# Squares of the first norm on ScalarE, a logarithm in two parts, and another order of small tasks at the entry of a recurrence

## The chip, the cores and the metric

The kernel runs on one core of a Trainium2 chip. The metric is the device time of one execution in microseconds (us). The core has five engines with instruction queues of their own: TensorE (PE, matmuls), VectorE (DVE), ScalarE (ACT), GpSimd (POOL) and SyncE (SP, which here issues DMAs). They wait for one another through semaphores.

## The reference, cut to what matters

512 tokens and 16 meta tokens, 1024 wide, pass through two blocks in float32. What the change touches lies at the start of the first block and in the second one:

```python
h = rmsnorm(h_res, norm1_w[l])              # x * rsqrt(mean(x * x) + eps) * w
proj = h @ w_in[l]                          # q, k, v, z, b, a, ...
qkv = silu(depthwise_conv_centred(concat([q, k, v]), conv_w))   # 5 taps
beta = sigmoid(b_raw)
g = -exp(A_log) * softplus(a_raw + dt_bias) # log decay, needs log(1 + exp(-|.|))
# gated delta rule, forward and backward, chunks of tokens, 8 heads:
#   v_new = u - w S;  o = q_dec S + (q k^T * decay) v_new;  S = S * exp(g_last) + k_dec^T v_new
...
u = causal_depthwise_conv(a_val * sigmoid(a_glu), conv_w, conv_b)   # 31 taps, second block
d = pooled differences of b_val, times pool_w; yb = d * pool_scale * silu(b_gate)
```

## The kernel before

Tokens lie in the free dimension, channels in the 128 partitions. A weight "unit" is 8 tiles of 128x128. For each, SP loads w_raw, ACT rounds it to w_hi (`round_unit`, L384), POOL computes the remainder w_lo (`split_unit`, L390), and PE makes three products with the activations' own hi and lo parts (`gemm`, L402). Four units are in flight.

First norm: the products of units 0 and 1 (tiles k0, k1) use the unnormalized x times the norm's weight, u_hi and u_lo. POOL squares the tiles 0 to 2 of x (L2431), ACT the tiles 3 to 7 (L1743), DVE first makes u_lo (L2085) and then adds the squares (L2092), PE takes the mean (L1447) and then the lo products (L425). ACT takes the root (L1748), DVE the reciprocal (L2097); units 0 to 3 are scaled afterwards (`scaled`, L2104). For units from 4 on, DVE makes the normalized rows (`first_row`, L2107), ACT rounds them into hp_hi (`first_hi`, L1754) and POOL makes hp_lo (`first_lo`, L2436). ACT does k = 4 to 7 of these at the start of its step n = 3, POOL likewise.

Tile loop: 24 tiles of q, k and v, a unit each. For tile n ACT copies the product into cacc with the first tap (L1772), DVE adds four taps (L2124), ACT applies silu (L1763). The dictionary `SIDE` names small tasks for each step n, done by every engine that has a part in them: the gates' decay (`gd`, DVE's log1p, L1227 to L479), decay sums (`dk`, L1477), transposes of k and v (`kt`, `vt`), exponentials of a chunk pair (`pg`) and its key and query products (`pk`), meta tokens' state (`msa`, `msb`), parts of a triangular inverse on DVE (`sub`, L610, L613, L616). A chunk pair is half the heads of one chunk, 8 pairs in all. The results of `pg` and `pk` go through DRAM (`sp_pk`: d_at, d_kc, d_qd, d_p) because SBUF is full; the next `pg` on the buffer waits until the store has landed (`spilled`).

Recurrence: 16 slots, forward and backward in turn. A slot loads its matrices (L1026 to L1049), doubles the inverse (`pe_t`, `pe_yx`, `pe_y64`), multiplies by the state (`pe_ks`), solves (`pe_w`, L919, after DVE's `dve_r` and `dve_yc64`) and updates (`pe_ds`). Pairs 5 to 7 are prepared inside slots 0 to 2 (`PREP`). The order on each engine is the order in the program text.

Second block: DVE runs the 31-tap filter in 248 steps (L1218), spread by hand between other work: `BV_STEPS` after each tile of the pooled branch, five ahead of each of four pairs of yb (L2341), and `BG_STEPS` ahead of each tile of the bgate product.

Of the kernel before, what the change touches and what calls it, by code (L numbers as in the profile page):

```python
# [14 lines left out]
KT = D // P  # L15
# [4 lines left out]
H = 8  # L20
# [19 lines left out]
SQP = 3  # L40
# [19 lines left out]
BV_STEPS = [4, 4, 3, 15, 7, 10, 14, 34]  # L60
BG_STEPS = [6, 6, 6, 5, 5, 5, 0, 0]
# [7 lines left out]
for _name, _n, _k in PARAMS:  # L69
# [13 lines left out]
SIDE = {1: [("ba", 0)], 2: [("bat", 0)], 3: [("gd", 0)], 4: [("kt", 0)], 5: [("kt", 1), ("dk", 0)],  # L83
# [7 lines left out]
        24: [("pg", 4), ("vt", 3), ("vtm", 3), ("pkp", 4), ("msa", 1), ("msb", 1), ("pk", 4)]}  # L91
# [35 lines left out]
def build(nc, a, out):  # L127
    ctx = ExitStack()
    with ctx:
# [190 lines left out]
        sq = Signal(sem("s_sq"), n1=KT - SQP, q=H, z=H, out=KT, down=2 * KT, va=KT, mix=KT, lout=KT)  # L320
# [22 lines left out]
        pw = Signal(sem("s_pw"), n1=SQP, s=sum(j // 2 + 2 for j in range(4, KT)))  # L343
# [126 lines left out]
        def dve_gd(e):  # L470
            t = [tmpc[:, i, :] for i in range(4)]
            t0 = t[0].rearrange("p (c n) -> p c n", c=NB)
            ea = small[:, 32:48].unsqueeze(1).to_broadcast([P, NB, 16])
            e.wait_ge(*ga.at("ex", 1))
            n = log1p(e, dg, "ch", 3, t[1], t[2], t[3])
            e.scalar_tensor_tensor(t[0], t[0], 0.0, t[1], ALU.max, ALU.add).then_inc(dg.sem, 1)
            e.wait_ge(*dg.at("ch", n + 1))
            e.wait_ge(*ga.at("eA", 1))
            e.scalar_tensor_tensor(gdec[:], t0, -1.0, ea, ALU.mult, ALU.mult).then_inc(dg.sem, 1)  # L479
            for _ in range(20 - n - 2):  # L480
                e.sem_inc(dg.sem, 1)
# [742 lines left out]
        def log1p(e, sig, part, n, y, t1, t2):  # L1224

            c = [2.0 / (2 * k + 1) for k in range(SERIES)]
            e.tensor_scalar(t1, y, 2.0, None, ALU.add).then_inc(sig.sem, 1)  # L1227
            e.wait_ge(*sig.at(part, n + 1))
            e.reciprocal(t2, t1).then_inc(sig.sem, 1)
            e.wait_ge(*sig.at(part, n + 2))  # L1230
            e.tensor_tensor(y, y, t2, ALU.mult).then_inc(sig.sem, 1)
            e.wait_ge(*sig.at(part, n + 3))
            e.tensor_tensor(t1, y, y, ALU.mult).then_inc(sig.sem, 1)
            e.wait_ge(*sig.at(part, n + 4))
            e.tensor_scalar(t2, t1, c[SERIES - 1], None, ALU.mult).then_inc(sig.sem, 1)
            n += 5
            for k in range(SERIES - 2, 0, -1):
                e.wait_ge(*sig.at(part, n))
                e.scalar_tensor_tensor(t2, t2, c[k], t1, ALU.add, ALU.mult).then_inc(sig.sem, 1)
                n += 1  # L1240
            e.wait_ge(*sig.at(part, n))
            e.scalar_tensor_tensor(y, t2, c[0], y, ALU.add, ALU.mult).then_inc(sig.sem, 1)
            e.wait_ge(*sig.at(part, n + 1))
            return n + 1
# [188 lines left out]
        def pe_program(e):  # L1433
# [5 lines left out]
            for n in range(len(TILES) + 1):  # L1439
# [18 lines left out]
                for task, arg in SIDE.get(n, ()):  # L1458
# [27 lines left out]
                    if task == "pg":  # L1486
                        pe_pg(e, arg)
# [15 lines left out]
            pe_t(e, 0, 0, 32)  # L1503
            pe_yx(e, 0, 0)
            pe_t(e, 0, 0, 64)
            for q, (s, k) in enumerate(SLOTS):
                nx = SLOTS[q + 1] if q < 15 else None
                if q in PREP:
                    pe_pg(e, PREP[q])
                pe_ks(e, s, k)  # L1510
                pe_y64(e, s, k)
                if nx:
                    pe_t(e, *nx, 32)
                if q in ZAT:
                    pe_z(e, ZAT[q])
                if q in SCA:
                    pe_c(e, SCA[q])
                if q in SCB:
                    pe_b(e, SCB[q])
                if q in (10, 12):  # L1520
                    pe_on(e, q - 10)
                pe_w(e, s, k)
                if nx:
                    pe_yx(e, *nx)
                if q in ZAT:
                    pe_z(e, ZAT[q] + 1)
                if q in SCA:
                    pe_x(e, SCA[q])
                if q == 8:
                    pe_on_sum(e, 0)  # L1530
                if q in (10, 12):
                    pe_on(e, q - 9)
                if q in PREP:
                    pe_pk(e, PREP[q])
                pe_ds(e, s, k)
                if nx:
                    pe_t(e, *nx, 64)
# [193 lines left out]
        def act_program(e):  # L1731
# [4 lines left out]

            round_unit(e, 0)
# [4 lines left out]
            for k in range(SQP, KT):  # L1742
                e.activation(sqv[:, k, :], x_in[:, k, :], ACT.Square).then_inc(sq.sem, 1)  # L1743
# [3 lines left out]
            e.wait_ge(*dg.at("halo", 9))  # L1747
# [9 lines left out]
            for n in range(len(TILES) + 2):  # L1757
# [6 lines left out]
                if n < len(TILES):  # L1764
                    what, h = TILES[n]
                    b = 2 * (n % 2)
                    for k in ((), (), (0, 1, 2), (4, 5, 6, 7))[n] if n < 4 else ():
                        first_hi(k)
# [4 lines left out]
                    if n == 2:  # L1773
                        first_hi(3)
# [40 lines left out]
            act_tc(e, 0, 0, 32)  # L1815
            act_xc(e, 0, 0)
            act_tc(e, 0, 0, 64)
            for q, (s, k) in enumerate(SLOTS):
                nx = SLOTS[q + 1] if q < 15 else None
                act_kd(e, s, k)  # L1820
                if q in PREP:
                    act_pg(e, PREP[q])
# [4 lines left out]
                if nx:  # L1827
                    act_tc(e, *nx, 32)
                if q in ZAT:
                    act_z(e, ZAT[q])  # L1830
# [244 lines left out]
        def dve_program(e):  # L2075
# [10 lines left out]
            e.wait_ge(*pw.at("n1", 1))  # L2086
            for k in range(1, KT):
                e.wait_ge(*(pw.at("n1", k + 1) if k < SQP else sq.at("n1", k - SQP + 1)))
                if k > 1:
                    e.wait_ge(*ad.at("n1", k - 1))  # L2090
                s = pair(sqv[:, 0, :]) if k == 1 else ps[:, 6:8, 0:HALF]
                e.tensor_tensor(pair(cacc[:, 0, :]) if k == KT - 1 else ps[:, 6:8, 0:HALF], s, pair(sqv[:, k, :]), ALU.add).then_inc(ad.sem, 1)  # L2092
# [19 lines left out]
            for n in range(len(TILES) + 1):  # L2112
# [21 lines left out]
                for task, arg in SIDE.get(n, ()):  # L2134
                    if task == "bat":
                        dve_bat(e)
                    if task == "gd":
                        dve_gd(e)
# [14 lines left out]

            dve_yc32(e, 0, 0)
            for q, (s, k) in enumerate(SLOTS):
                nx = SLOTS[q + 1] if q < 15 else None
                if q in PREP:
                    dve_pg(e, PREP[q])
                dve_r(e, s, k)
                dve_yc64(e, s, k)  # L2160
                if q in (4, 5):
                    sub_part(e, 1, 3 * (q - 4) + 1)
                dve_vn(e, s, k)
                if q in SCB:
# [5 lines left out]
                if q in PREP:  # L2170
                    dve_pk(e, PREP[q])
# [3 lines left out]
                dve_o(e, s, k)  # L2175
                if q in (3, 4, 5):
# [89 lines left out]
            n = log1p(e, dg, "lam", 3, t[1], t[2], t[3])  # L2266
# [160 lines left out]
        def pool_program(e):  # L2427
            split_unit(e, 0)
            for k in range(SQP):
                e.wait_ge(s_x[k // 2], 16 if k > 1 else 32)  # L2430
                e.tensor_tensor(sqv[:, k, :], x_in[:, k, :], x_in[:, k, :], ALU.mult).then_inc(pw.sem, 1)  # L2431
# [7 lines left out]
            for n in range(len(TILES) + 1):  # L2439
                if n == 3:  # L2440
                    for k in range(4, KT):
                        first_lo(k)
                if n < len(TILES):
                    split_unit(e, n + 2)
                if n == 2:
                    for k in range(4):
# [12 lines left out]
            e.memset(oT[:], 0.0).then_inc(pz.sem, 1)  # L2459
            for q, (s, k) in enumerate(SLOTS):  # L2460
# [234 lines left out]
```

## Time and profile before

| | |
|---|---|
| three runs | 1849.55, 1853.29, 1853.92 us |
| median | 1853.29 us |
| the profiled execution | 1849.43 us, of which the span is 1847.6 us |
| mean granted PE clock | 0.972 of full speed |
| PE busy | 1755.8 us (95% of the span) |
| DVE busy | 842.5 us (46%) |
| ACT busy | 667.1 us (36%) |
| POOL busy | 866.8 us (47%) |

PE is the busiest engine by far, and the chain of work that ended last is PE's for 74% of the span. Idle time of another engine costs nothing unless PE, or a chain that PE hangs on, waits for it. A clock of 0.5 in a stretch means that PE's matmuls run at 1.2 instead of 2.4 GHz there.

### The profile page before, as it was taken

What the parts mean: (1) busy time and instruction counts of PE and PEld (TensorE: products, weight loads), DVE (VectorE), ACT (ScalarE), POOL (GpSimd) and SP (SyncE); (2) the same over time, 40 slices, a digit from 0 to 9 for tenths busy, and PEclk for the clock granted to TensorE, in tenths of its full rate; (3) what the DMA queues carried; (4) which work ended last, traced back from release to release, by engine and by line L of the source; (5) the groups of instructions that cost most, each with busy time, mean ns of one, the idle gap of its engine ahead of it and who ended that gap; (6) DMA issues with size and microseconds to landing.
All of it is one profiled execution on the core that took longest, in us unless ns stands there. A gap on an engine that the chain in (4) does not pass through costs nothing.

```text
span 1847.6 us, 22825 instructions
## 1 busy us (share of the span) xinstructions
PE 1755.8 (95%) x9151; PEld 1478.5 (80%) x9151; DVE 842.5 (46%) x1338; ACT 667.1 (36%) x978; POOL 866.8 (47%) x485
## 2 busy tenths in 40 slices
PE   7799979999999999999999999989999999999987
PEld 7789878898998888877888878868887788877766
DVE  7677944833433300222111121128999933357732
ACT  5456533333232322234222232232233244356551
POOL 4345533322333644544555554444477445456552
PEclk9899978999999999999999999989999989999999
DMA  4367267454322224322322223323233222222222
GB/s 172 101 207 214 75 179 217 135 157 135 121 86 77 96 91 137 95 95 85 101 93 91 93 90 103 102 68 103 92 91 103 80 69 90 88 97 92 92 69 80
DMA packets 120145, 201.41 MB, mean 109 GB/s; under 512 B 32448, under 2 KB 71512, under 8 KB 120040
## 3 DMA queue, kind: packets, MB, share of 16 engines
q1 hardware_dynamic: 118552, 197.47, 33.6%
q10 hardware_dynamic: 1488, 2.48, 0.4%
q8 instruction: 73, 1.20, 0.3%
q14 instruction: 32, 0.26, 0.0%
HBM read 170.46 MB, written 29.46 MB: 108 GB/s over the span
## 4 chain that ended last, share of the span: by engine, by line
PE 74%; DVE 6%; POOL 2%; issue 2%; ACT 1%; DMA 0%; SPq 0%; DVEq 0%; ACTq 0%; POOLq 0%
PE ps L402 60%; PE ps L1723 3%; DVE ps L1218 2%; PE ps L873 1%; POOL w_lo L390 1%; PE ps L919 1%; PE ps L883 1%; POOL tmp L2524 1%; PE ps L881 1%; PE ps L926 1%; PE ps L913 1%; PE ps L930 1%; PE ps L905 1%; PE ps L891 1%; DVE ps L1337 1%
## 5 line engine op out<-in xcount | busy, mean ns | idle before, releaser
L390 POOL TENSOR_TENSOR w_lo<-w_raw,w_hi 128x1024 fp32r<-128x1024 f32 x264 | 634.4, 2411 | 574.5 <-ACT w_hi L384 574.2
L402 PE MATMUL ps<-hp_hi,w_hi 128*128 128x512 f32 (+2 forms) x1664 | 557.1, 362 | 3.8 <-DVE cacc L2124 1.5
L402 PE MATMUL ps<-hp_lo,w_hi 128*128 128x512 f32 (+2 forms) x1664 | 552.0, 359 | 0.0
L402 PE MATMUL ps<-hp_hi,w_lo 128*128 128x512 f32 (+2 forms) x1664 | 551.8, 359 | 0.0
L402 PEld LDWEIGHTS ps<-hp_hi,w_hi 128*128 128x128 f32 x1664 | 296.5, 190 | 60.2 <-issue 7.9
L384 ACT ACTIVATE w_hi<-w_raw 128x1024 fp32r<-128x1024 f32 x264 | 277.8, 1054 | 172.2 <-DMA w_raw<-in_w 164.1
L402 PEld LDWEIGHTS ps<-hp_lo,w_hi 128*128 128x128 f32 x1664 | 296.1, 189 | 50.4 <-issue 1.7
L402 PEld LDWEIGHTS ps<-hp_hi,w_lo 128*128 128x128 f32 x1664 | 296.0, 189 | 48.1
L1218 DVE SCALAR_TENSOR_TENSOR ps<-u_in,par,ps 128x511 f32<-128x511 f32 (+14 forms) x240 | 177.3, 739 | 7.7
L2124 DVE SCALAR_TENSOR_TENSOR cacc<-ps,par,cacc 128x528 f32<-128x528 f32 x96 | 73.6, 767 | 42.1 <-ACT cacc L1772 39.4
L2503 POOL TENSOR_TENSOR y_lo<-tmp,y_hi 128x512 fp32r<-128x512 f32 x22 | 28.4, 1290 | 105.6 <-ACT y_hi L1917 105.6
L402 PE MATMUL ps<-y_hi,w_hi 128*128 128x512 f32 x176 | 69.6, 396 | 1.5 <-DVE tmp L2255 1.5
L402 PE MATMUL ps<-y_lo,w_hi 128*128 128x512 f32 x176 | 69.5, 395 | 0.0
L402 PE MATMUL ps<-y_hi,w_lo 128*128 128x512 f32 x176 | 69.5, 395 | 0.0
L1914 ACT ACTIVATE tmp<-tmp 128x512 f32<-128x512 f32 x22 | 13.9, 632 | 150.6 <-DVE tmp L2248 150.6
L402 PE MATMUL ps<-mx_hi,w_hi 128*128 128x512 f32 x144 | 59.2, 411 | 4.8 <-DVE yb L2341 4.8
L2250 DVE TENSOR_TENSOR ps<-ps,tmp 128x512 f32<-128x512 f32 x22 | 15.4, 699 | 103.8 <-PE ps L402 103.8
L402 PE MATMUL ps<-mx_lo,w_hi 128*128 128x512 f32 x144 | 58.5, 406 | 0.0
L402 PE MATMUL ps<-mx_hi,w_lo 128*128 128x512 f32 x144 | 58.3, 405 | 0.0
L2248 DVE TENSOR_TENSOR tmp<-tmp,ps 128x512 f32<-128x512 f32 x22 | 15.1, 687 | 92.4 <-PE ps L402 85.7
L1008 POOL TENSOR_TENSOR KC<-st,tabs 128x512 f32<-128x512 f32 x16 | 16.9, 1053 | 84.3 <-PE ps L905 71.4
L2277 DVE TENSOR_TENSOR x<-x,ps 128x512 f32<-128x512 f32 x8 | 5.5, 686 | 102.2 <-PE ps L402 102.2
(397 smaller groups left out, 2602.8 us busy)
## 6 DMA issues: line engine op xcount, KB each, us to landing
w_raw<-in_w SPq DMA_DIRECT2D x264, 512.0 KB, 3.5
d_y<-zero SPq DMA_DIRECT2D x6, 688.0 KB, 6.0
d_x<-zero SPq DMA_DIRECT2D x6, 688.0 KB, 5.9
d_at<-at SPq DMA_DIRECT2D x16, 256.0 KB, 3.1
d_kc<-kc SPq DMA_DIRECT2D x16, 256.0 KB, 3.2
d_qd<-eg SPq DMA_DIRECT2D x16, 256.0 KB, 3.2
d_p<-dec SPq DMA_DIRECT2D x16, 256.0 KB, 3.3
AT<-d_at SPq DMA_DIRECT2D x16, 256.0 KB, 6.2
```

Source lines behind the costliest of these rows:

```text
L384: e.activation(w_hi[:, u % RAW, :], w_raw[:, u % RAW, :], ACT.Copy).then_inc(s_hi, 1)
L390: e.tensor_tensor(w_lo[:, u % RAW, :], w_raw[:, u % RAW, :], w_hi[:, u % RAW, :].bitcast(F32), ALU.subtract).then_inc(s_lo, 1)
L402: mm = e.matmul(ov, w, r[:, k, t0:t1], start=(first and n == 0 and p3 == 0), stop=(last and n == len(tiles) - 1 and p3 == 2))
L873: mm = e.matmul(bankv(LB[s], P, P)[:, u], SQ[s]["AT"][:, u], SQ[s]["X"][:, u], start=True, stop=True)
L881: e.matmul(half_cols(LB[s], 0)[:, u], T[:, u], blocks(Y, 1 - s)[:, u], start=True, stop=True)
L883: mm = e.matmul(half_cols(LB[s], 1)[:, u], Y[:, u], blocks(T, s)[:, u], start=True, stop=True)
L891: mm = e.matmul(bankv(LB[s], P, 64)[:, u], T[:, u], Y[:, u, c], start=True, stop=True)
L905: mm = e.matmul(bankv(QBK[s], P, P)[:, u], SQ[s]["KC"][:, u], S[:, u], start=True, stop=True)
L1218: e.scalar_tensor_tensor(acc[:, t:SEQ], u_in[:, k, 0:SEQ - t], w, acc[:, t:SEQ], ALU.mult, ALU.add).then_inc(cl.sem, 1)
L1723: mm = e.matmul(ps[:, LBANK[j], :], w, r[:, k, :], start=(k == 0 and p3 == 0), stop=(k == LT - 1 and p3 == 2))
L2124: e.scalar_tensor_tensor(acc, ps[:, b:b + 2, t:t + HALF], pcol(QKV[what][0], h, t), acc, ALU.mult, ALU.add).then_inc(cv.sem, 1)
L2503: e.tensor_tensor(y_lo[:, j - 1, :], row(2 + (j - 1) % 2), y_hi[:, j - 1, :].bitcast(F32), ALU.subtract).then_inc(lo.sem, 1)
```

## The change

1. The three squares on POOL go; ACT squares all eight tiles. ACT does a square root of one column at its very start, and no longer waits for DVE's clearing ahead of the real root.
2. DVE's log1p for the gates is cut in two: five operations (`log1p_ratio`, task `gda`) at step 3, and the rest (`log1p_series` and two more, task `gdb`) at step 4 behind the transposes' copies `kt`. The logarithm of lambda in the second block calls both, one behind the other.
3. ACT rounds hp_hi 3 to 7 in one go in step 2, POOL makes hp_lo 0 to 7 in one go in step 2.
4. Of pair 4's tasks at step 24 only PE's part of `pg` stays. The other engines' parts, `pk`, `msa` and `msb` of the second half are spread over the first operations of the recurrence.
5. In slots 0 to 2 the preparation of pairs 5 to 7 (`pg`, `pk`) moves behind the slot's own operations on PE, ACT and DVE. SP's order is the same.
6. `BV_STEPS` has 28 instead of 34 steps for the last tile; `BG_STEPS` has six more, in tiles 3, 4 and 6 as the lists show.

```diff
-BV_STEPS = [4, 4, 3, 15, 7, 10, 14, 34]
-BG_STEPS = [6, 6, 6, 5, 5, 5, 0, 0]
+BV_STEPS = [4, 4, 3, 15, 7, 10, 14, 28]
+BG_STEPS = [6, 6, 6, 6, 6, 5, 4, 0]
-SIDE = {1: [("ba", 0)], 2: [("bat", 0)], 3: [("gd", 0)], 4: [("kt", 0)], 5: [("kt", 1), ("dk", 0)],
+SIDE = {1: [("ba", 0)], 2: [("bat", 0)], 3: [("gda", 0)], 4: [("kt", 0), ("gdb", 0)], 5: [("kt", 1), ("dk", 0)],
...
-        24: [("pg", 4), ("vt", 3), ("vtm", 3), ("pkp", 4), ("msa", 1), ("msb", 1), ("pk", 4)]}
+        24: [("pgp", 4), ("vt", 3), ("vtm", 3)]}
...
+        def dve_gda(e):
+            e.wait_ge(*ga.at("ex", 1))
+            log1p_ratio(e, dg, "ch", 3, tmpc[:, 1, :], tmpc[:, 2, :], tmpc[:, 3, :])
+        def dve_gdb(e):
...
+            n = log1p_series(e, dg, "ch", 8, t[1], t[2], t[3])
...
             pe_t(e, 0, 0, 32)
+            pe_msa(e, 1)
             pe_yx(e, 0, 0)
+            pe_msb(e, 1)
             pe_t(e, 0, 0, 64)
...
-                if q in PREP:
-                    pe_pg(e, PREP[q])
+                if q == 0:
+                    e.wait_ge(*m_st.at(1))
                 pe_ks(e, s, k)
+                if q == 0:
+                    pe_pk(e, 4)
                 pe_y64(e, s, k)
...
                 pe_w(e, s, k)
+                if q in PREP:
+                    pe_pg(e, PREP[q])
...
+                pe_ds(e, s, k)
                 if q in PREP:
                     pe_pk(e, PREP[q])
-                pe_ds(e, s, k)
...
+            e.wait_ge(*dg.at("halo", 9))
+            e.activation(rrow[:, 0:1], rrow[:, 0:1], ACT.Sqrt)
             round_unit(e, 0)
...
-            for k in range(SQP, KT):
+            for k in range(KT):
                 e.activation(sqv[:, k, :], x_in[:, k, :], ACT.Square).then_inc(sq.sem, 1)
...
-                    for k in ((), (), (0, 1, 2), (4, 5, 6, 7))[n] if n < 4 else ():
+                    for k in (0, 1, 2) if n == 2 else ():
                         first_hi(k)
...
                     if n == 2:
-                        first_hi(3)
+                        for k in range(3, KT):
+                            first_hi(k)
...
             act_tc(e, 0, 0, 32)
+            act_msa(e, 1)
             act_xc(e, 0, 0)
+            act_msb(e, 1)
+            act_pg(e, 4)
             act_tc(e, 0, 0, 64)
...
+            dve_pg(e, 4)
             dve_yc32(e, 0, 0)
...
                 dve_r(e, s, k)
+                if q == 0:
+                    dve_pk(e, 4)
                 dve_yc64(e, s, k)
...
                 dve_vn(e, s, k)
+                if q in PREP:
+                    dve_pg(e, PREP[q])
...
                 dve_s(e, s, k)
                 dve_o(e, s, k)
+                if q in PREP:
+                    dve_pk(e, PREP[q])
...
-            for k in range(SQP):
-                e.wait_ge(s_x[k // 2], 16 if k > 1 else 32)
-                e.tensor_tensor(sqv[:, k, :], x_in[:, k, :], x_in[:, k, :], ALU.mult).then_inc(pw.sem, 1)
...
                 if n == 2:
-                    for k in range(4):
+                    for k in range(KT):
                         first_lo(k)
...
             e.memset(oT[:], 0.0).then_inc(pz.sem, 1)
+            pool_pk(e, 4)
```

## Rows read from the trace of the kernel before

**Rows 1.** Waits of PE, whole span: engine, line, waited for: us, times, longest.

```profile
PE ps L637 <- ACT qT L1763: 6.2, 1, 6.2
...
PE ps L402 <- DVE yb L2341: 5.7, 2, 4.8
...
PE ps L417 <- ACT hp_hi L1754: 4.6, 1, 4.6
PE ps L1447 <- DVE cacc L2092: 4.6, 1, 4.6
```

**Rows 2.** Windows, PE first in each row; PEclk is the granted clock.

```profile
22.00:26.00 4.00, 2.51 (x7) 0.60 0.00 0
...
82.00:86.00 4.00, 4.00 (x18) 0.50 0.00 0
...
110.00:200.00 90.00, 86.98 (x681) 79.96 (x681) 68.40 (x139) 50.82 (x71) 50.14 (x47) 0.99 0.63 192
```

**Rows 3.** One line's instructions, u_lo on DVE: durations min/median/max in ns.

```profile
L2085 DVE SCALAR_TENSOR_TENSOR u_lo<-x_in,par,u_hi x8: 756/1508/2902, 7.0 to 17.0; 128x528 fp32r<-128x528 f32 x8
```

**Rows 4.** Timeline of the first 32 us: start us, us, engine, line, operation.

```profile
13.40 2.76 ACT L1743 ACTIVATE sqv<-x_in 128x528 f32<-128x528 f32 x5
...
13.57 2.98 POOL L390 TENSOR_TENSOR w_lo<-w_raw,w_hi 128x1024 fp32r<-128x1024 f32 x1 [1.20 <-ACT w_hi L384]
...
18.53 4.00 DVE L2092 TENSOR_TENSOR ps<-ps,sqv 128x528 f32<-128x528 f32 x5
...
23.49 2.10 PE L1447 MATMUL ps<-cacc,cf 128*128 128x264 f32 x4 [4.61 <-DVE cacc L2092]
...
25.01 6.40 PE L425 MATMUL ps<-u_lo,w_hi 128*128 128x268 f32 x32
```

**Rows 5.** Timeline from 47 to 91 us.

```profile
47.98 2.78 DVE L2107 SCALAR_TENSOR_TENSOR hf<-x_in,par,ps 128x528 f32<-128x528 f32 x4
...
51.15 0.27 ACT L1786 ACTIVATE beta<-beta 128x80 f32<-128x80 f32 x1 [4.39 <-DVE beta L463]
...
55.37 0.64 ACT L1763 ACTIVATE kT<-cacc 128x528 f32<-128x528 f32 x1
...
58.76 3.18 DVE L2124 SCALAR_TENSOR_TENSOR cacc<-ps,par,cacc 128x528 f32<-128x528 f32 x4 [6.35 <-ACT cacc L1772]
61.86 2.40 DVE L1227 TENSOR_SCALAR tmpc<-tmpc 128x80 f32<-128x80 f32 x1
...
64.15 4.76 POOL L390 TENSOR_TENSOR w_lo<-w_raw,w_hi 128x1024 fp32r<-128x1024 f32 x2
...
69.28 1.90 DVE L1239 SCALAR_TENSOR_TENSOR tmpc<-tmpc 128x80 f32<-128x80 f32 x7
...
75.91 1.94 PE L637 MATMUL ps<-cf,kT 128*128 128x128 f32 x8 [6.24 <-ACT qT L1763]
77.65 0.90 PE L1477 MATMUL ps<-gdec,cf 128*128 128x32 f32 x4
...
90.63 0.60 PE L643 MATMUL ps<-cf,kT 128*16 128x128 f32 x4
```

**Rows 6.** Timeline where the tiles pass into the recurrence, 238 to 315 us.

```profile
238.90 1.03 DVE L616 COPY raw<-inv 128x1024 f32<-128x1024 f32 x1
...
249.68 0.38 SPq L1029 DMA_DIRECT2D X<-d_x  x1
...
252.22 1.13 DVE L560 SCALAR_TENSOR_TENSOR at<-ps,b,dec 128x128 f32<-128x128 f32 x4 [10.22 <-ACT st L840]
...
252.79 2.05 PE L873 MATMUL ps<-X,AT 128*128 128x128 f32 x8 [1.24 <-issue]
...
283.31 1.13 DVE L522 SCALAR_TENSOR_TENSOR dec<-ps,tabs,cf 128x128 f32<-128x128 f32 x4 [3.39 <-DMA d_p<-dec]
...
285.63 2.04 PE L919 MATMUL ps<-TR,Y 128*128 128x128 f32 x8 [3.61 <-DVE Y L974]
...
314.82 0.48 PE L402 MATMUL ps<-hp_hi,w_hi 128*128 128x512 f32 x1
```

**Rows 7.** Timeline of DVE near the end of the bval tiles, 31-tap filter.

```profile
1421.47 10.16 DVE L1218 SCALAR_TENSOR_TENSOR ps<-u_in,par,ps 128x511 f32<-128x511 f32 x13
```

## What I predict, and why

> **What bounds the kernel now.** I first read the page: TensorE (PE) is busy 95% of the span, so time can only come from PE's remaining waits and from stretches where its clock is low. Then the view of PE's waits, longest first [rows 1]. The reader is to see that three of its long waits lie in the places this change touches: 4.6 us for the sum of the first norm's squares, 4.6 us for hp_hi and 6.2 us for a silu near 75 us, and that a fourth, 5.7 us in two pieces for yb near 1433, lies where the step lists act. Then the timeline of each engine around each wait, and the windows for PE's clock. In between PE is the bound: from 110 to 200 us it works 86.98 of 90 us [rows 2], so what is won ahead of it arrives as a shift of all that follows. The sum is made on the profiled execution, 1849.4 us; the median shown is 1853.3, with one run at 1849.6, so the profile is one of the quicker executions.
>
> **1. First norm's squares on ACT.** Removed: three squares on POOL; each of them stretches the u_lo operations beside it on DVE from 0.76 to about 1.5 us, and the last one, beside POOL's w_lo(1), takes 2.90 [rows 3]. So DVE finishes u_lo near 17.7 and only then adds. Added: three squares on ACT at 2.76 / 5 = 0.55 us. All eight begin at 13.40 [rows 4]; the second is ready at 14.5, the eighth at 17.8. u_lo without POOL follows ACT and is done near 13.3. The adds come every 0.80 us (4.00 / 5) and need seven: from 14.5 they would end at 20.2. The first add reads two SBUF tensors while POOL writes w_lo(1) from about 13.5 to 15.9. If it is held to the end, the last add ends near 20.9; before, PE got it at 23.49 [rows 4]. Gain 2.4 to 3.1; I take 2.4, because u_lo's 2.90 shows such a hold. The Trainium skill (GPSIMD Engine Reference, section 8, Key points) says that GpSimd shares its SBUF interfaces with VectorE and contends with its instructions that have two SBUF inputs; by that rule the sum takes 2.4, without it 3.1, and the trace agrees with the rule (0.76 against 2.90).
> PE's gap before the mean also shrinks, from 4.6 to about 2.2 us. Before, its clock stood at 0.60 in 22 to 26 us [rows 2], the four mean matmuls took 2.10 and the 32 lo matmuls 6.40 [rows 4]; at the full level I estimate half of the one and 4.0 for the other. PE then runs without a gap to 51.9, so it could win 3.4 more, but DVE's chain (root, reciprocal, first tap) only moves by the mean's 1.0 and then by what PE hands it, about 2.0 in all. Full clock: 4.4. I take **-4.0** (ends -2.2 and -4.6). The early square root moves a table load to a place where ACT waits for its first DMA: nothing, and the load's old place was inside ACT's wait for the mean.
>
> **2. Logarithm in two parts, hp_hi and hp_lo in one run.** In the times of before: DVE's rows for k = 4 to 7 are there by 50.8 [rows 5]. ACT now rounds them at once, by 51.4, and POOL's four remainders end near 53.8 instead of 61. PE's unit 4 then needs no wait: 49.8 to 55.9. Its 4.6 us go, but unit 5 needs tile 3's taps, so what is late next is DVE's tile 3. Its price: ACT starts the sigmoid after 51.4 plus a table load, 52.7; from there to the silu took 4.22 us (51.15 to 55.37), so the silu is at 56.9, the copy into cacc at 57.5, DVE's taps from 58.2 to 61.3 instead of 58.76 to 61.9. Unit 5 starts at 61.35 rather than 63.46, after a gap of 4.4 us and so at the low clock at first: I let it end at 69.0.
> DVE then: before, the log's first operation waited 2.40 us for POOL [rows 5], and the whole took 61.86 to 71.99. Now w_lo(6) is over by 61.5, w_lo(7) begins near 63.6, and the five operations of the first part (0.2 us or so each, 0.65 for the reciprocal) fit in between: 63.1. Taps of tile 4 to 66.2, two copies into k_tok (1.28) to 67.5, the second part's ten operations at 0.27 (7 in 1.90) to 70.2. PE's transposes of kt(1) wait for those copies, which are now there before unit 5 ends, and run behind it to 70.0 instead of starting at 75.91 [rows 5]; its decay sums start at 70.2 instead of 77.65. They and unit 6 took until 90.5, at clock 0.50 [rows 2, 5]: 4.6 and 8.4 us. At the full level I estimate 2.5 and 6.1, so unit 6 ends at 78.8; at the low level throughout, 83.2. Gain 7.2 to 11.7. PE has worked since 61.35, so I take **-10.5**. Behind unit 6 ACT, DVE and POOL are free sooner as well, and the weight loads are tied to PE's own signals, so the whole is a shift.
>
> **3. Order of small tasks.** Pair 4's key products, the memory state of the second half (msa, msb) and their ACT, DVE and POOL parts leave the end of the tile loop. But the recurrence starts on its transfers: X is issued at 249.68 behind the scatters and PE starts at 252.79 on it [rows 6]; the scatters hang on DVE's last copy of the substitution, 238.90 to 239.9 [rows 6], which the change leaves alone. So the moved work was in a cover that now stays empty, for 13 us. What it costs inside: msa(1) and msb(1) fall in PE's waits for ACT, 0.2 us. DVE's four operations of pk(4), two groups of four at 1.13 us [rows 6] and two products of some 0.7, together 3.75, now stand between r and yc64 of slot 0, so W of slot 0 waits from about 269.1 to 273.2, against 269.3 before: +3.9. SP's eight stores of pair 4 wait for them too (256 to 262 before, 270 to 275 now), and behind them SP's loads of slot 2, needed 10 us later, and the P buffer that DVE's next dec waits for. Against this, PE's pg(5) to pg(7), DVE's pk and POOL's pk now come at the end of their slots, so r and yc64 of the next slot are released by the pk in front of them: slot 1's W waited 3.61 us, and ran at 2.04 us for eight instead of some 1.1, because dec waited 3.39 us for d_p [rows 6]. I followed the slots with these durations: with PE at the full level the z products, at 314.82 before [rows 6], start 2.3 us sooner; if the 4.1 us wait drops the clock for some ten us, as after 285.63, 1.9 later. Every wait of that length in the trace was followed by the low level. I take **+1** (ends -3 and +6, for a spill landing late once more). The Trainium skill (TensorE: Matmul & The Clock Gate, HAM oscillation) describes a loop in which each wait between bursts returns the array to half rate; by it the term is +1.9.
>
> **4. Steps of the 31-tap filter.** Six steps leave the eighth bval tile for the later bgate ones. Behind them DVE produces yb, on which PE waits 4.8 and 0.9 us. A step costs 10.16 / 13 = 0.78 us [rows 7], six 4.7; DVE is the bound from there to the first bgate unit. The steps reappear where DVE waited 2 to 5 us per tile for ACT (from 1472 on), so their cover holds; tile 7's sum, due when PE ends bgate 7, is done some 6 us ahead. **-4.6** (ends -2.6, if bgate 0 now runs at the low clock after the shorter waits, and -4.8). The split logarithm of lambda has the same operations: nothing.
>
> **Sum.** -4.0 - 10.5 + 1 - 4.6 = -18.1 on 1849.4 gives 1831.3. Since the shown median stands higher than its profile, I forecast 1833.
>
> **Rivals.** (a) The clock does not come back: the mean, the decay sums and unit 6 stay at 1.2 GHz, as in 82 to 86 us [rows 2], and slot 0's stall lowers it again: -2.4 for part 1, -7.2 for 2, +3 for 3 and -3 for 4 are -9.6, so with the same 1.7 for the median 1841.5. For it: the decay sums are tiny matmuls, in which the clock stayed low before. Against it: no gap stands before them now. (b) The first part of the logarithm misses its window between w_lo(6) and w_lo(7), by 0.5 us or more, and is again held some 2.4 us, and once more by what follows: -18.1 + 5 gives 1838. The margin is thin. (c) The entry becomes the bound: each of slots 0 to 2 pays what slot 1 did before (stall 3.6, low clock about 5), slot 0 also its pk(4) (3.8) and the moved products at the low clock (about 5.7), and the spills of P land late, 4.6 us in each. That is some 26 + 10 less the one stall that was there (8.7), plus 14: 41 at the very worst; the other parts give 19.1, so it decides from 19.1 + 5.6 = 24.7 us on, and at 30 it gives 1862. For it: slot 1 shows the pattern. Against it: in slots 0 and 2 as they were, the same waits stayed below 1 us. (d) The log's gain stays but the filter's is taken by the next wait: yb's wait only moves to a bgate unit, 1838.
>
> **Chances.** Forecast 0.50, (a) 0.22, (b) 0.13, (c) 0.04, (d) 0.06, more gain than forecast 0.05. The likeliest case alone reaches from 1825 to 1838; the range with (a) and (b), and 2 us for which execution is the median, is 1823 to 1844. 0.3% of the time is 5.6 us, about what a measurement can tell from none. Faster by more 0.92, within 0.05, slower 0.03.
>
> **What would show it.** Adds begin near 14.5 and the mean near 21; no wait of PE inside unit 4; a wait of some 4 us in front of unit 5; log operations in two groups with none over 1 us; decay sums some 11 us earlier (7.5 and part 1's shift); PE idle from about 240 to 252 less the shift; a wait of W in slot 0 near 4 us; the wait for yb under 2.5 us in each piece. The prediction is wrong if a w_lo holds a log operation, if the clock stays low through unit 6, or if the slots behind 252 take over 6 us more.

## The result, and the profile after

The changed kernel takes 1831.9 us in the median (1831.81 to 1837.01, 4 runs), the kernel before 1851.4 (1849.54 to 1853.92, 4 runs): ratio 0.9901, 95% interval 0.9878 to 0.9924. The profiled execution took 1831.8 us, its span is 1830.0 us at a mean granted clock of 0.976. Predicted were 1833 us and a range of 1823 to 1844. Four more executions of the same kernel on a later occasion had a median of 1837.3 beside 1852.6 for the kernel before, so the gain is 19.5 us by the first occasion and 15.3 by the second. Both occasions hold executions near 1832 and near 1837 us; what lies between these two figures is told below.

PE's waits of the changed kernel, longest first (engine, line, waited for: us, times, longest), answer to [rows 1]:

```profile
PE ps L875 <- issue: 12.8, 1, 12.8
...
PE ps L921 <- DVE Y L976: 6.2, 4, 4.0
PE ps L401 <- DVE cacc L2137: 6.1, 2, 4.7
...
PE ps L401 <- DVE yb L2360: 3.5, 2, 2.1
...
PE ps L1450 <- DVE cacc L2105: 3.3, 1, 3.3
```

The wait for hp_hi in unit 4 and the one for the silu near 75 us are gone. New are 4.7 us in front of unit 5 (cacc) and 4.0 us in slot 0 (Y), both foretold. The wait for the mean has gone from 4.6 to 3.3 us, the one for yb from 5.7 to 3.5.

First norm, timeline of the changed kernel, against [rows 3, 4]:

```profile
6.76 6.53 DVE L2099 SCALAR_TENSOR_TENSOR u_lo<-x_in,par,u_hi 128x528 fp32r<-128x528 f32 x8 [4.69 <-ACT u_hi L1751]
...
12.96 4.37 ACT L1754 ACTIVATE sqv<-x_in 128x528 f32<-128x528 f32 x8
13.14 2.43 POOL L389 TENSOR_TENSOR w_lo<-w_raw,w_hi 128x1024 fp32r<-128x1024 f32 x1 [5.17 <-ACT w_hi L383]
14.16 1.99 DVE L2105 TENSOR_TENSOR ps<-sqv 128x528 f32<-128x528 f32 x1 [0.86 <-ACT sqv L1754]
...
21.21 1.72 PE L1450 MATMUL ps<-cacc,cf 128*128 128x264 f32 x4 [3.32 <-DVE cacc L2105]
22.35 5.54 PE L424 MATMUL ps<-u_lo,w_hi 128*128 128x268 f32 x32
```

The eight u_lo take 6.53 us where they took over 10. The first add begins at 14.16 and is held to 16.15, past the end of POOL's w_lo(1) at 15.57: the hold that I had taken. The same add took 0.70 us in the kernel before, where it ran from 17.72 with POOL idle. The mean starts at 21.21 instead of 23.49.

Units 5 and 6, timeline of the changed kernel, against [rows 5]:

```profile
55.71 2.35 POOL L389 TENSOR_TENSOR w_lo<-w_raw,w_hi 128x1024 fp32r<-128x1024 f32 x1 [0.24 <-ACT w_hi L383]
...
57.81 0.30 DVE L1228 TENSOR_SCALAR tmpc<-tmpc 128x80 f32<-128x80 f32 x1
57.95 0.81 PE L401 MATMUL ps<-hp_hi,w_hi 128*128 128x268 f32 x2 [4.67 <-DVE cacc L2137]
...
59.39 0.20 DVE L1236 TENSOR_SCALAR tmpc<-tmpc 128x80 f32<-128x80 f32 x1
...
63.79 1.89 DVE L1242 SCALAR_TENSOR_TENSOR tmpc<-tmpc 128x80 f32<-128x80 f32 x7
...
66.08 1.04 PE L639 MATMUL ps<-cf,kT 128*128 128x128 f32 x8
66.96 0.53 PE L1480 MATMUL ps<-gdec,cf 128*128 128x32 f32 x4
...
75.59 0.60 PE L645 MATMUL ps<-cf,kT 128*16 128x128 f32 x4
```

The first part of the logarithm (57.81 to 59.59) starts 0.25 us before w_lo(6) is over (58.06) and ends 0.6 us before w_lo(7) begins (60.19). The decay sums start at 66.96 instead of 77.65, 10.7 us sooner. The transposes behind unit 6 start at 75.59 instead of 90.63. Windows of the changed kernel (PE, its weight loads, DVE, ACT, POOL; then granted clock, DMA share, GB/s), against [rows 2]:

```profile
22.00:26.00 4.00, 4.00 (x22) 3.79 (x21) 2.50 (x3) 0.70 (x1) 0.00 (x0) 0.62 0.02 4
56.00:64.00 8.00, 6.05 (x32) 6.05 (x33) 7.69 (x15) 2.83 (x4) 4.43 (x2) 0.59 0.23 84
64.00:90.00 26.00, 25.93 (x209) 25.43 (x207) 16.50 (x33) 16.91 (x24) 4.77 (x2) 1.00 0.49 142
```

The granted clock is 1.00 (2.4 GHz) in all of 64 to 90 us, through decay sums and unit 6, where it had been at 0.50 (1.2 GHz) from the decay sums at 77.65 to near 88 us, in unit 6.

The entry of the recurrence, PE's timeline, against [rows 6]:

```profile
237.35 2.05 PE L875 MATMUL ps<-X,AT 128*128 128x128 f32 x8 [12.75 <-issue]
239.32 1.89 PE L818 MATMUL ps<-v_met,m_dec 16*16 16x128 f32 x8
...
244.74 2.07 PE L828 MATMUL ps<-v_met,k_met 16*128 16x128 f32 x8
...
251.21 1.06 PE L507 MATMUL ps<-kT 128*128 128x128 f32 x8
252.10 1.06 PE L512 MATMUL ps<-qT,kT 128*128 128x128 f32 x8
...
258.92 2.05 PE L921 MATMUL ps<-TR,Y 128*128 128x128 f32 x8 [3.98 <-DVE Y L976]
260.76 3.48 PE L498 MATMUL ps<-cf,gdec 128*128 128x128 f32 x16
...
274.52 1.13 PE L921 MATMUL ps<-TR,Y 128*128 128x128 f32 x8 [0.45 <-DVE Y L976]
...
287.58 1.13 PE L921 MATMUL ps<-TR,Y 128*128 128x128 f32 x8 [0.32 <-DVE Y L976]
...
300.08 0.48 PE L401 MATMUL ps<-hp_hi,w_hi 128*128 128x512 f32 x1
```

PE idles for 12.75 us, starts 15.4 us sooner than before (252.79), loses 3.98 in slot 0, and no longer the 3.61 of slot 1. L818 and L828 are PE's moved msa(1) and msb(1), L507 and L512 its moved products of pair 4. The z products start 14.7 us sooner.

DVE's 31-tap filter ahead of yb, and PE's two waits behind it, timelines of the changed kernel, against [rows 7]:

```profile
1406.78 5.47 DVE L1220 SCALAR_TENSOR_TENSOR ps<-u_in,par,ps 128x511 f32<-128x511 f32 x7
...
1418.95 0.50 PE L401 MATMUL ps<-mx_hi,w_hi 128*128 128x512 f32 x1 [2.14 <-DVE yb L2360]
...
1423.41 0.50 PE L401 MATMUL ps<-hp_hi,w_hi 128*128 128x512 f32 x1 [1.40 <-DVE yb L2360]
```

Seven steps stand where 13 did (10.16 us). The first bgate unit starts 19.3 us sooner than before (1442.73).

Of these 19.3 us only 17.6 reach the end. The loss of 2.1 us has one place (0.4 is won back in small pieces behind it): 64 matmuls of one column each (the variance of a later norm, L1670 before, L1679 after). They took 9.41 us from 1509.79 before and take 11.53 now:

```profile
1490.44 11.53 PE L1679 MATMUL ps<-cf,tmp 128*128 128x1 f32 x64
```

PE is busy all the while; only the clock differs. Windows there, columns as above, first of the kernel before, then of the changed one:

```profile
1512.00:1514.00 2.00, 2.00 (x20) 2.00 (x19) 0.00 (x0) 0.00 (x0) 0.00 (x0) 1.00 0.31 125
1514.00:1516.00 2.00, 2.00 (x13) 2.00 (x12) 0.00 (x0) 0.00 (x0) 0.00 (x0) 0.61 0.03 8
```

```profile
1492.00:1494.00 2.00, 2.00 (x15) 2.00 (x14) 0.00 (x0) 0.00 (x0) 0.00 (x0) 0.69 0.62 242
1494.00:1502.00 8.00, 7.97 (x38) 7.88 (x37) 0.00 (x0) 0.00 (x0) 0.00 (x0) 0.50 0.01 2
```

The clock falls about 5 us into the group before, and less than 3 us into it after.

### The profile page after: what moved, and what is told of

Read it like the earlier page. It is cut to its first block, busy times and chain, and to the rows that moved or that the text cites. A ratio compares the mean times of both kernels' runs of the same rounds, so it can differ in the third digit from the quotient of the medians.

```text
span 1830.0 us, 22824 instructions
## 1 busy us (share of the span) xinstructions
PE 1744.6 (95%) x9151; PEld 1469.1 (80%) x9151; DVE 836.0 (46%) x1338; ACT 668.1 (37%) x981; POOL 861.5 (47%) x482
## 4 chain that ended last, share of the span: by engine, by line
PE 80%; DVE 11%; ACT 3%; issue 2%; POOL 2%; DMA 1%; SPq 0%; DVEq 0%; ACTq 0%; POOLq 0%
PE ps L401 63%; PE ps L1732 3%; DVE cacc L2137 2%; DVE ps L1220 2%; PE ps L875 2%; POOL w_lo L389 1%; PE ps L921 1%; POOL tmp L2538 1%; DVE inv L615 1%; PE ps L928 1%; PE ps L885 1%; PE ps L907 1%; PE ps L883 1%; PE ps L915 1%; PE ps L932 1%
## 5 line engine op out<-in xcount | busy, mean ns | idle before, releaser
L2268 DVE TENSOR_TENSOR ps<-ps,tmp 128x512 f32<-128x512 f32 x22 | 15.4, 699 | 103.9 <-PE ps L401 103.9
L943 ACT ACTIVATE TR<-ps 128x512 f32<-128x512 f32 x32 | 19.1, 597 | 91.4 <-PE ps L875 91.4
```

The costliest lines, as they stand in the source:

```text
L943: e.activation(SQ[s]["TR"][:], bankv(LB[s], P, P), ACT.Copy).then_inc(q_tc[s].sem, 1)
```

## The experiments

A shift is how much sooner the same PE instruction starts than in the kernel before, in two profiled executions. Some shift can stand there already ahead of the part in question, where the clock rose or fell at another point; where it matters it is given too. Each part alone on the kernel before came first (the kernel before had 1852.6 us there, 28 runs, 1848.19 to 1859.09).

**Squares alone.** The whole first part of the change: ACT squares all eight tiles, POOL none, and the early square root is in.

```diff
+            e.wait_ge(*dg.at("halo", 9))
+            e.activation(rrow[:, 0:1], rrow[:, 0:1], ACT.Sqrt)
...
-            for k in range(SQP, KT):
+            for k in range(KT):
                 e.activation(sqv[:, k, :], x_in[:, k, :], ACT.Square).then_inc(sq.sem, 1)
...
-            for k in range(SQP):
-                e.wait_ge(s_x[k // 2], 16 if k > 1 else 32)
-                e.tensor_tensor(sqv[:, k, :], x_in[:, k, :], x_in[:, k, :], ALU.mult).then_inc(pw.sem, 1)
```

> The kernel before with the first part of the change alone (all eight squares on ACT, early square root). Theory A (POOL's three squares stretched u_lo and so the sum of squares, and the shorter gap lets PE's clock come back sooner): the mean's products start near 21.2 instead of 23.49, unit 2 near 33.7 instead of 37.2, and the 3.5 us pass through to the end: ratio near 0.998. Rival: the shift is eaten by PE's next wait, for hp_hi inside unit 4, which grows from 4.6 to about 8 us, and the time stays as before.

Measured: 1847.65 us, ratio 0.9972 (0.9959 to 0.9986). Mean at 21.20, all that follows 3.7 us sooner up to unit 4, where the wait for hp_hi grows from 4.6 to 5.4 us. From there to the decay sums the shift is 2.5 to 3.0 us, and behind unit 6 it is 4.1, since the clock came back 1 us sooner there. So hp_hi takes about 0.8 us and not the whole; how much of the 3.7 is left behind it, 2.5 to 4.1 us, depends on the clock. Squares and early square root were not taken apart.

**hp in one run, alone, and the logarithm cut in two, alone.**

```diff
-                    for k in ((), (), (0, 1, 2), (4, 5, 6, 7))[n] if n < 4 else ():
+                    for k in (0, 1, 2) if n == 2 else ():
...
-                        first_hi(3)
+                        for k in range(3, KT):
+                            first_hi(k)
...
-                if n == 3:
-                    for k in range(4, KT):
-                        first_lo(k)
...
-                    for k in range(4):
+                    for k in range(KT):
                         first_lo(k)
```

The second one calls the two halves of the function as in the change:

```diff
-3: [("gd", 0)], 4: [("kt", 0)],
+3: [("gda", 0)], 4: [("kt", 0), ("gdb", 0)],
```

> The kernel before with hp_hi 3 to 7 and hp_lo 0 to 7 each in one run in step 2, the logarithm whole. Theory A (the logarithm was slow because POOL's w_lo(6) and w_lo(7) ran beside it; moving POOL's remainders forward takes them apart): no wait in unit 4, the logarithm takes some 4.5 us instead of 10.1, the decay sums start at 71 to 72 instead of 77.65, gain 9 to 11 us, ratio near 0.995. Rival B (the cut of the logarithm is what gains): only the earlier unit 5 is won, some 2 us, ratio 0.999, with log operations still over 1.5 us.

> The kernel before with the logarithm cut in two alone. Theory A: the first part still meets w_lo(6) and w_lo(7) and is held as before (operations of 1.6 to 2.4 us), only the second part leaves the way of tile 4's taps; the decay sums start 0 to 3 us sooner, ratio 0.998 to 1.000. Rival B: the decay sums start near 70, gain 8 us or more, ratio 0.995.

hp alone: 1845.05 us, ratio 0.9956 (0.9938 to 0.9974), shift 6.5 us behind unit 6, of which 0.3 stood there ahead of unit 4, so 6.2 by the part: less than the 9 to 11 expected. The first part of the logarithm is free (0.20 to 0.65 us an operation), but the whole now runs on in one piece, and its series of seven falls beside the next w_lo, as DVE and POOL of this kernel show:

```profile
62.88 3.94 DVE L1239 SCALAR_TENSOR_TENSOR tmpc<-tmpc 128x80 f32<-128x80 f32 x7
...
63.44 2.45 POOL L390 TENSOR_TENSOR w_lo<-w_raw,w_hi 128x1024 fp32r<-128x1024 f32 x1 [2.13 <-ACT w_hi L384]
```

Seven operations take 3.94 us instead of 1.89. And it still stands ahead of tile 4's taps and, behind them, the first copy into k_tok, on which PE's transposes wait 1.78 us. (The profile puts this wait down to qT, which ends at about the same time; by the program, L635, it is the copy.)

The cut alone: 1848.07 us, ratio 0.9978 (0.9964 to 0.9991), decay sums 2.6 us sooner, as expected, and 2.5 behind unit 6; ahead of unit 4 a shift of 1.2 had stood there, which is no work of this part. DVE of this kernel shows why no more:

```profile
60.66 2.41 DVE L1229 TENSOR_SCALAR tmpc<-tmpc 128x80 f32<-128x80 f32 x1
63.11 0.65 DVE L1231 RECIPROCAL tmpc<-tmpc 128x80 f32<-128x80 f32 x1
63.79 1.68 DVE L1233 TENSOR_TENSOR tmpc<-tmpc 128x80 f32<-128x80 f32 x1
65.50 2.31 DVE L1235 TENSOR_TENSOR tmpc<-tmpc 128x80 f32<-128x80 f32 x1
```

Three of the first part's five operations are held by POOL, which works from 59.72 (w_lo(6)) to 67.7 with little pause since its hp_lo came late.

**Both together, without the rest** (both diffs above).

> The kernel before with the logarithm cut in two and with hp_hi and hp_lo in one run, nothing else. Theory A (the two halves need each other: the merged hp work frees POOL, so the first part of the logarithm is no longer held, and the cut lets the second part run behind the copies of kt): log operations of the first part under 0.7 us each, decay sums near 70, unit 6 over near 79, 10 to 12 us sooner than before, ratio 0.994. Rival B (the halves only add, as they were run alone: 6.2 and 2.5 us): decay sums near 69 to 72 and 8 to 9 us, ratio 0.9955. Rival C (the surplus came from the first norm's earlier end): the shift behind unit 6 is at most 9 us, with a POOL subtraction beside the first part.

1840.78 us (1836.64 to 1845.09, 6 runs) against 1852.28, ratio 0.9936 (0.9922 to 0.9950). First part 60.87 to 62.65 without a hold, series at 66.84 in 1.89 us, decay sums at 70.25, shift behind unit 6 10.2 us. Singly the shifts were 6.5 and 2.5, together 9.0; less what stood there ahead of unit 4 (0.5 here, 0.3 and 1.2 there) it is 9.8 against 6.2 + 1.3 = 7.5. So the two halves give 1.2 to 2.3 us more together than one by one. That is theory A, at its lower edge: B's ratio of 0.9955 lies outside the interval, and no log operation is over 0.7 us. C's 9 us is passed by little. In this execution the clock was still at 0.79 in 72 to 80 us. In the first profile of the full change it was 1.00 and the part gave 11.5; in the repeat told below, the same program, it gave 9.6, so this difference lies in the clock of the execution and not in the other parts.

**Step lists alone.**

```diff
-BV_STEPS = [4, 4, 3, 15, 7, 10, 14, 34]
-BG_STEPS = [6, 6, 6, 5, 5, 5, 0, 0]
+BV_STEPS = [4, 4, 3, 15, 7, 10, 14, 28]
+BG_STEPS = [6, 6, 6, 6, 6, 5, 4, 0]
```

> The kernel before with the two step lists alone. Theory A (DVE's filter steps hold yb, and yb holds PE): the first bgate unit starts 4.6 us sooner, of which 0 to 2.1 us are given back where the one-column products of the variance run longer at the low clock; ratio 0.9975 to 0.9986. Rival D (the wait only moves into a later bgate unit): ratio 1.000.

1848.95 us, ratio 0.9981 (0.9968 to 0.9994). The first bgate unit gains 4.6 us on the kernel before. In this execution that only makes up for 4.6 us lost ahead of it, most of it by clock falls near 550 to 590 us, so the unit starts at the same time in both. The waits for yb are 3.5 instead of 5.7 us; the other 2.4 us lie in PE's work there, at which the clock now stays at 1.00:

```profile
1428.00:1440.00 12.00, 9.73 (x41) 1.00 0.55 176
```

The same window of the kernel before is at 0.72. The one-column products begin at 1509.72, at the same time as before (1509.79), and take 10.81 us instead of 9.41: 1.4 us is given back.

The next four were timed beside one another, and so beside the changed kernel itself, whose median was 1837.3 us there (the kernel before had 1852.6, 7 runs):

**The old entry.** All of the third part undone, the rest of the change kept.

> The changed kernel with the old order of small tasks at the entry of the recurrence (pair 4 whole at the end of the tile loop, preparation of pairs 5 to 7 ahead of the slots' own work). Theory A (the new order loses about as much with pair 4 in slot 0 as it wins in slot 1): the first z products at the same time within 1.5 us, the wait of W in slot 0 gone, that in slot 1 back at some 3.6 us with the low clock behind it; time within 1.5 us of the changed kernel. Rival C (the entry costs): 3 us or more quicker than the changed kernel. Rival E (the entry is where part of the gain comes from): 3 us or more slower.

1835.09 us (1832.22 to 1839.29), ratio 0.9902 (0.9879 to 0.9924). From the transposes of v ahead of the entry (223.18 in the changed kernel) to the z products it takes 0.9 us less than the changed kernel. PE waits again 3.62 us in slot 1 and 1.28 in slot 2, but not in slot 0. Theory A holds by the trace: the third part as a whole moves the z products by less than a microsecond. The medians, 1835.09 against 1837.3, can't tell so little.

**Pair 4 back in its cover.** Only SIDE[24] and pair 4's tasks are as before; pairs 5 to 7 keep the new order in their slots.

```diff
-        24: [("pgp", 4), ("vt", 3), ("vtm", 3)]}
+        24: [("pg", 4), ("vt", 3), ("vtm", 3), ("pkp", 4), ("msa", 1), ("msb", 1), ("pk", 4)]}
...
-            pe_msa(e, 1)
             pe_yx(e, 0, 0)
-            pe_msb(e, 1)
...
-                if q == 0:
-                    pe_pk(e, 4)
...
```

The parts of ACT, DVE and POOL go back in the same way.

> The changed kernel, but pair 4's exponentials and products and the second half's memory state go back to the end of the tile loop; the new order for pairs 5 to 7 stays. Theory A: the work lies in the 12.8 us in which PE waits for the recurrence's first load, slot 0 has no wait of 4 us and no low clock behind it, and slot 1 keeps its gain: the first z products start 5 to 8 us sooner, time 1824 to 1827 us. Rival F (pair 4's stores and loads collide with the slots' loads, or its DVE work delays the first load): the first load lands later, or dec waits for its buffer, and no more than 2 us are won.

1825.72 us (1824.87 to 1829.53), ratio 0.9860 (0.9841 to 0.9879): the quickest kernel of this study, 6 us ahead of the changed one's first median and 11.6 ahead of the one beside it. PE's timeline of this version:

```profile
242.04 2.08 PE L875 MATMUL ps<-X,AT 128*128 128x128 f32 x8
...
255.78 1.13 PE L921 MATMUL ps<-TR,Y 128*128 128x128 f32 x8 [0.32 <-DVE Y L976]
...
268.98 1.13 PE L921 MATMUL ps<-TR,Y 128*128 128x128 f32 x8 [0.45 <-DVE Y L976]
...
294.54 0.48 PE L401 MATMUL ps<-hp_hi,w_hi 128*128 128x512 f32 x1
```

No W waits over half a microsecond, and from X to z are 52.5 us instead of 62.7 (300.08 - 237.35). PE works 6.41 us of 226 to 238 where the changed kernel works 0.65. From the transposes of v to z it is 9.3 us quicker than the changed kernel, and 8.5 quicker than the old entry. So the third part is two changes of opposite sign: the new order of pairs 5 to 7 in their slots saves 8.5 us, and taking pair 4 out of its cover costs 9.3 (with the new order in place; without it this was not run).

The rows of both kernels say where the 9.3 us go. The wait of W in slot 0 is 3.98 instead of 0.32 us (3.7). Slot 0 behind it, to the next W, runs 2.4 us longer, because the clock is low from that wait to 264 us. The moved msa(1) and msb(1) take 3.8 us at 1.2 GHz and fill waits of 1.5 that stood at their places (2.3). The moved products of pair 4 take 1.8 us, at full clock. Against this, the first doubling (X) comes 0.9 us sooner.

**Three steps back** into the eighth bval tile (31, with six, six, six, six, six, six and no others in the bgate list).

> The changed kernel with 31 instead of 28 filter steps behind the last bval tile (three fewer behind). Theory A: the first bgate unit starts 3 x 0.77 = 2.3 us later than in the changed kernel. If the one-column products for the variance are then not caught earlier by the low clock, part or all of it comes back: they take 9.4 to 11.5 us, so the time is 0.2 to 2.5 us longer than the changed kernel's. Rival D: no change in the first bgate unit, the wait was taken up elsewhere.

1834.31 us (1833.61 to 1838.38), ratio 0.9907 (0.9888 to 0.9926): not told apart from the changed kernel in time. In the trace the waits for yb are 4.6 us instead of 3.5, the first bgate unit starts 4.8 us later, of which 2.5 already stood there from clock falls, so 2.3 by the three steps, as expected, and the one-column products take 10.16 us, between those of the two lists.

**The changed kernel once more.**

> The changed kernel once more, beside the others on the same chip. Theory A and all rivals: 1832 us; the products for the variance near 11.5 us where the profile is like the first one, and another length wherever the clock falls at another point.

1837.3 us (1832.8 to 1837.69), ratio 0.9913 (0.9894 to 0.9932); its profile has a span of 1835.6 us, 5.6 more than the first. Compared instruction by instruction with the first, the difference arises in pieces: 1.6 us before 28 us, 1.9 in the decay sums and unit 6, 0.8 near 216, 1.2 between 250 and 300, 0.3 behind. Windows of the first execution and of this one (PE busy, granted clock, DMA share, GB/s):

```profile
72.00:76.00 4.00, 4.00 (x36) 1.00 0.00 0
212.00:220.00 8.00, 7.31 (x59) 1.00 0.13 40
```

```profile
72.00:76.00 4.00, 4.00 (x22) 0.59 0.40 149
212.00:220.00 8.00, 6.63 (x40) 0.79 0.15 61
```

The same program, the same matmuls, and a clock that falls in one execution and not in the other.

**ACT's gate operations behind tile 3**, on the version with pair 4 in its cover: the sigmoid and the two exponentials of step 2 go to step 3, behind the copy of tile 3 into cacc.

```diff
-                    if task == "bat":
+                    if task == "gda":
                         e.wait_ge(*dg.at("b", 1))
                         e.activation(beta[:], beta[:], ACT.Sigmoid).then_inc(ga.sem, 1)
```

> The version that keeps pair 4 in its cover, and ACT's three gate operations (a sigmoid, two exponentials, with two table loads) behind the copy of tile 3 into cacc instead of ahead of it. Theory A (the wait of 4.7 us in front of unit 5 hangs on ACT's gate operations, and what is late next is the second part of the logarithm): no wait in front of unit 5; PE waits some 2 to 4 us for k_tok and the decay sums instead; decay sums 2 to 3 us sooner; end 1822 to 1824 against 1826. Rival B (the table loads are not what unit 5 waits for, or w_lo is held instead): the wait stays above 3 us and the time is the same. Rival C (the first part of the logarithm now falls beside the subtraction of w_lo and is held 2 us): decay sums no sooner, 1826 or later.

1826.62 us (1825.36 to 1830.92), ratio 0.9858 (0.9843 to 0.9872) on a third occasion, so no gain is seen on pair 4 in its cover (1825.72). PE's and DVE's rows of this version:

```profile
55.45 0.52 PE L401 MATMUL ps<-hp_hi,w_hi 128*128 128x268 f32 x2 [2.09 <-DVE cacc L2128]
...
56.69 2.32 DVE L1234 TENSOR_TENSOR tmpc<-tmpc 128x80 f32<-128x80 f32 x1
...
63.07 1.23 PE L639 MATMUL ps<-cf,kT 128*128 128x128 f32 x8 [1.37 <-ACT qT L1767]
66.21 1.06 PE L1480 MATMUL ps<-gdec,cf 128*128 128x32 f32 x4 [1.92 <-DVE gdec L481]
```

Unit 5's wait falls from 4.7 to 2.1 us and it starts 3.8 us sooner than with pair 4 in its cover (1.2 of which stood there already), so just over half of the wait did hang on ACT's gate operations. But one operation of the first part is held 2.32 us by w_lo(6), PE waits 1.4 and 1.9 us further on, and the decay sums start 2.3 us sooner, but behind them the clock is low again (their first four matmuls take 1.06 us, at full clock 0.53): by 75 us both versions are level, and the 1.2 us that stood there are lost too. The wait was split, not removed. C came nearest, with its hold and its time, though the decay sums do start sooner.

## Why the prediction came out right, point by point

**Sum.** Predicted -18.1 on the profiled 1849.4, measured -17.6. By terms: part 1 -3.5 for -4.0, part 2 -11.5 for -10.5, part 3 +0.3 for +1, part 4 -4.6 for -4.6, then +2.1 that no term had, and -0.4 in small pieces behind. The forecast of 1833 lies between the medians of the two occasions, 1831.9 and 1837.3. That the sum is met within 0.5 us is in part luck: its terms are off by +0.5, -1.0, -0.7, 0, +2.1 and -0.4, which cancel, and in the repeat parts 1 and 2 gave 2.0 and 9.6 instead of 3.5 and 11.5, with the same program.

**Part 1** was right in its mechanism. The 3.1 us that the sum of squares would give without a hold did not come: 2.28 did, for the 2.4 taken. About 0.4 of them are the execution's: ACT began its squares at 12.96 instead of 13.40. In the five profiles with the old first norm the mean starts at 23.47 to 23.54, in the seven with the new one at 21.14 to 22.03. By the Trainium skill (GPSIMD Engine Reference, section 8, Key points), POOL contends with VectorE instructions that have two SBUF inputs; the trace agrees, with 1.99 us for the first add beside w_lo(1) and 0.70 for the same add with POOL idle in the kernel before. PE's gap before the mean shrank to 3.3 us only and not to 2.2, because PE's work ahead of it ended 1.0 us sooner as well. The half microsecond missing lies in the clock, which came back later in the lo products (5.54 us) than I had counted.

**Part 2** was right in each step: no wait in unit 4; 4.67 us in front of unit 5 (4.4 predicted); log operations of at most 0.65 us; transposes of kt(1) directly behind unit 5; decay sums 10.7 us sooner (11 predicted). The size lay near the upper end because the clock was at its full level from 64 us on; in four of the other profiles of both halves it fell once more in unit 6, and the part gave 9.6 to 9.8 us. The price of -10.5 lies between the two. Rival (b), the missed window, did not occur in the full change, but its mechanism is real: the cut alone has three operations held, hp alone a series at twice its time, and the kernel with ACT's gate operations behind tile 3 one operation of 2.32 us. In the full change the first part ends 0.6 us ahead of w_lo(7).

**Part 3** was right as a sum, and in part by luck: W of slot 0 waits 3.98 us (about 4 predicted), the clock falls with it (2.05 us for eight matmuls) and slot 1's wait is gone. What I had not priced well is the two halves. I worked out 2.3 us in favour at full clock; the runs show 8.5 of gain and 9.3 of cost. The gain is that slot 1's stall (3.2), its low clock (4.4) and most of the 1.28 of slot 2 (1.0) all go. In the cost, msa(1) and msb(1) were priced at 0.2 us and cost 2.3 net, at 1.2 GHz behind an idle stretch of 12.75 us (2.07 us for eight), while the clock's fall in the new wait of W cost 2.4 for the 4.2 that lie between the two cases of the forecast (-2.3 and +1.9). Rival (c), an entry that becomes the bound, did not occur: W waits 0.45 and 0.32 us in slots 1 and 2.

**Part 4** was right to the tenth for the first bgate unit (4.6, from 14.7 to 19.3 us of shift), and the steps' new places cost nothing that a row shows. Rival (d) was wrong as put, since no bgate wait took the gain.

**The term I did not have** is the 2.1 us at the one-column products, and it belongs to part 4. In the five kernels with the old lists the group takes 9.15 to 9.49 us, in the six profiles with the new lists 10.64 to 11.53, with three steps back 10.16, wherever it begins. In the kernels with the old lists the clock falls at the end of a wait for yb, in those with the new ones it stays at 1.00 there and falls sooner in the group. That the one fall delays the other is my reading of this pattern and not tested by itself. So the step lists are worth 4.6 less 1.4 to 2.1, some 2.5 to 3.2 us, which agrees with the 3.7 in the median of that part alone.

**Rival (a)**, a clock that doesn't come back, was wrong for unit 6 in the first profile; in the repeat the clock falls there once more, at a cost of 1.9 us with the decay sums. It is a matter of the execution, not of the kernel alone, and its 0.22 was not too much.

## What to carry to other kernels

A task that is taken out of an idle stretch and put between busy ones can cost its whole length and more, even where the order around it becomes better: here 9.3 us for 5.6 us of PE's work; when a change moves a stretch little, undo its parts one at a time and look for two that cancel. A short DVE operation beside a long POOL one can cost the rest of the POOL operation, so a chain of short ones is best cut where POOL pauses, and the pause must be made before the cut pays. A wait that two chains end within 2 us of each other is not won by speeding up one of them.

## What the runs showed of the hardware

**The clock falls in a fully busy PE.** In the one-column products PE shows 2.00 of 2.00 us busy in the windows around the fall, and the granted clock goes from 1.00 to 0.50, 2 to 5 us into the group. The same 64 matmuls take 9.15 to 11.53 us by when it falls. The Trainium skill (TensorE: Matmul & The Clock Gate, HAM oscillation) describes falls by waits between bursts; slot 0 agrees (3.98 us of wait, then 2.05 us for eight matmuls), but this fall comes with no wait at all.

**Executions of one kernel differ by such falls.** The repeat's span was 5.6 us longer with a clock of 0.973 instead of 0.976, in pieces of 1 to 2 us, as at 72 to 76 and 212 to 220 us, which are at full clock in the other execution. Effects below 4 us were therefore read from shifts in the trace up to a named instruction, not from medians.

**Single-input operations are held too.** The 128x80 TENSOR_SCALAR of the logarithm, with one SBUF input, took 2.41 us beside POOL's subtraction and the clearing behind it (59.72 to 63.01 us) in the kernel with the cut alone, 2.40 in the kernel before [rows 5], and 0.20 to 0.30 where POOL was idle or all but done. Not every one is: the RECIPROCAL behind it took 0.65 us beside POOL's next subtraction, which runs from 62.98, and the same 0.65 in the changed kernel, where POOL is idle. Why these two differ was not tried.
